# The shared expert's down product: in 32-column slices with every combine, or whole in the first round

## The reference, cut to what matters

```python
def moe(x, ...):                       # xt: 256 tokens x 1024
    ...                                # sigmoid scores, 8 of 64 experts for each token, gates
    # for each expert e, on the tokens that chose it:
    y = (silu(h @ w_gate[e]) * (h @ w_up[e])) @ w_down[e] * wt
    routed = segment_sum(y, token)
    shared = (silu(xt @ sh_gate) * (xt @ sh_up)) @ sh_down      # 256 x 256 @ 256 x 1024
    return routed + shared

x = layer_norm(ALPHA * x + moe(x), ln2_g[i], ln2_b[i])          # ALPHA = (2 * DEPTH) ** 0.25
```

## Time and profile before

| | before |
|---|---|
| time, median of 3 runs | 1450.87 us (1449.27 to 1454.12) |
| profiled execution | span 1450.8 us; the page gives no other time for it |
| TensorE busy with matmuls | 1404.1 us, 97% |
| TensorE weight loads | 875.4 us, 60% |
| VectorE busy | 555.3 us, 38% |
| ScalarE busy | 361.1 us, 25% |
| mean granted TensorE clock | 0.985 |
| DMA | 468.48 MB, mean 323 GB/s |

### The profile page before, as it was taken

One profiled execution on the slowest core, in us unless ns is written; L12 is line 12 of the kernel. 1 busy time (PEld: TensorE's weight loads), 2 busy tenths in 40 slices (PEclk: granted clock), 3 DMA queues, 4 the chain that ended last, 5 costly groups with the idle time before them and its releaser, 6 DMA issues.

```text
span 1450.8 us, 20457 instructions
## 1 busy us (share of the span) xinstructions
PE 1404.1 (97%) x7848; PEld 875.4 (60%) x7848; DVE 555.3 (38%) x1085; ACT 361.1 (25%) x611; POOL 10.2 (1%) x24
## 2 busy tenths in 40 slices
PE   8999999999999999995999999999999999999996
PEld 8986455555455555544999997455554555555553
DVE  5665232222233222234577666322222332222234
ACT  4422211122111112212544443121221111122110
POOL 0000000000000000000000000000000000000000
PEclk9999999999999999997999999999999999999998
DMA  9764799999999999964444455489999999999990
GB/s 332 269 262 200 305 384 396 403 394 394 410 392 392 397 399 401 398 232 186 175 175 160 173 238 205 157 333 387 393 397 405 383 410 398 389 399 396 392 378 30
DMA packets 82769, 468.48 MB, mean 323 GB/s; under 512 B 7065, under 2 KB 19481, under 8 KB 32674
## 3 DMA queue, kind: packets, MB, share of 16 engines
q1 hardware_dynamic: 81296, 463.50, 80.4%
q10 hardware_dynamic: 1426, 4.33, 0.8%
HBM read 466.76 MB, written 1.05 MB: 322 GB/s over the span
## 4 chain that ended last, share of the span: by engine, by line
PE 95%; DVE 2%; issue 1%; ACT 1%; DMA 0%; POOL 0%; DVEq 0%; POOLq 0%; ACTq 0%
PE ps L583 30%; PE ps L605 16%; PE ps L668 9%; PE ps L555 9%; PE ps L535 9%; PE ps L680 6%; PE ps L702 5%; PE ps L561 3%; PE ps L751 2%; PE ps L542 2%; PE ps L591 1%; PE ps L521 1%; PE ps L735 1%; PE ps L744 0%; DMA xT_in<-in_xT 0%
## 5 line engine op out<-in xcount | busy, mean ns | idle before, releaser
L583 PE MATMUL ps<-ring,xsT 128*64 128x512 f32 x2048 | 450.1, 592 | 1.2 <-DVE slot_tok L1053 1.2
L583 PEld LDWEIGHTS ps<-ring,xsT 128*64 128x64 f32 x2048 | 146.9, 137 | 292.6 <-issue 291.2
L605 PE MATMUL ps<-ring,hidT 128*64 128x512 f32 x1024 | 233.8, 598 | 2.3 <-ACT hidT L850 2.3
L996 DVE TENSOR_TENSOR ring_low<-ring,wh 128x1024 fp32r<-128x1024 f32 (+1 forms) x112 | 128.4, 1148 | 113.0 <-ACT wh L828 112.5
L1059 DVE SCALAR_TENSOR_TENSOR gated<-sig,slot_gate,ps 128x256 f32<-128x256 f32 x64 | 30.8, 481 | 364.7 <-ACT sig L846 364.7
L1068 DVE TENSOR_TENSOR yl<-ps,yh 128x512 fp32r<-128x512 f32 x128 | 88.5, 691 | 175.2 <-ACT yh L855 175.2
L828 ACT CAST wh<-ring 128x1024 fp32r<-128x1024 f32 (+1 forms) x112 | 110.5, 988 | 157.7 <-PE ps L668 70.6
L855 ACT CAST yh<-ps 128x512 fp32r<-128x512 f32 x128 | 75.0, 586 | 268.1 <-PE ps L605 268.1
L605 PEld LDWEIGHTS ps<-ring,hidT 128*64 128x64 f32 x1024 | 67.8, 136 | 114.5 <-issue 109.6
L535 PE MATMUL ps<-sel,xh 128*128 128x256 f32 x512 | 130.8, 296 | 4.3 <-DVE g_cols L1046 4.3
L846 ACT ACTIVATE sig<-ps 128x256 f32<-128x256 f32 x64 | 24.6, 384 | 401.8 <-PE ps L583 401.8
(11 more groups left out here) (149 smaller groups left out, 1418.8 us busy)
## 6 DMA issues: line engine op xcount, KB each, us to landing
ring<-in_w_gate SPq DMA_DIRECT2D x128, 1024.0 KB, 7.5
ring<-in_w_up SPq DMA_DIRECT2D x128, 1024.0 KB, 9.9
ring<-in_w_down SPq DMA_DIRECT2D x128, 1024.0 KB, 9.0
ring<-in_b_w_in SPq DMA_DIRECT2D x8, 3072.0 KB, 11.9
ring<-in_a_w_in SPq DMA_DIRECT2D x12, 1024.0 KB, 12.7
ring<-in_b_w_out SPq DMA_DIRECT2D x4, 3072.0 KB, 11.5
ring<-in_a_w_out SPq DMA_DIRECT2D x1, 3072.0 KB, 16.5
ring<-in_sh_gate SPq DMA_DIRECT2D x2, 1024.0 KB, 4.7
```

What stands on the lines that cost most here:

```text
L583: last = nc.tensor.matmul(ps[64 * half:64 * half + 64, p, :], xsT[:, c, (2 * p + half) * SLOTS:(2 * p + half + 1) * SLOTS], slot_gu(s)[:, ...
L605: last = nc.tensor.matmul(ps[64 * half:64 * half + 64, 4 + h, :], hidT[:, p, kk * P + 64 * half:kk * P + 64 * half + 64], slot_dn(s)[:, kk ...
L996: nc.vector.tensor_tensor(wl_n, w, wh_n.bitcast(FP32), ALU.subtract).then_inc(L[layer].wl_ready, 1)
```

## The change

The two 32-column products leave `combine`. Instead `shared_down(t)` computes, in round 0, 128 tokens x 1024 columns for each token half t, as four products of 512 columns (two column halves, two contraction steps) into PSUM banks 2 and 3: for t = 0 behind `down(0, 0)`, for t = 1 behind `slot_info` and ahead of `down(0, 1)`. The second waits for `acc_ready`, since it writes the same banks. VectorE then computes ALPHA * x + product for each half in one instruction over 1024 columns (`residual_and_shared`), both behind `select` and ahead of `take_info` in round 0. ScalarE's two scalings, the wait before round 1 and the memset go. The sums into `acc` are the same but for their order.

```diff
                                                     start=(p == 0 and part is yh),
-                                                    stop=(p == 1 and part is yl and not k.head_first))
-                    if k.head_first:
-                        for kk in range(HC):
-                            last = nc.tensor.matmul(ps[:, 2 + n % 2, bass.ds((i - 1) * SHARE, SHARE)],
-                                                    sh_hT[:, kk, t * P:(t + 1) * P],
-                                                    sh_dn[:, kk, bass.ds((i - 1) * SHARE + h * HALF, SHARE)],
-                                                    start=False, stop=(kk == HC - 1))
+                                                    stop=(p == 1 and part is yl))
                     last.then_inc(k.comb_done, 1)
...
+                def shared_down(t):
+                    if t == 0:
+                        pe.wait_ge(shared.sh_hT_ready, 1)
+                        pe.wait_ge(g.sh_dn, 16 * (k.layer + 1))
+                    else:
+                        pe.wait_ge(shared.acc_ready, t)
+                    for h in range(2):
+                        for kk in range(HC):
+                            last = nc.tensor.matmul(ps[:, 2 + h, :], sh_hT[:, kk, t * P:(t + 1) * P],
+                                                    sh_dn[:, kk, h * HALF:(h + 1) * HALF],
+                                                    start=(kk == 0), stop=(kk == HC - 1))
+                    last.then_inc(shared.sh_down, 1)
...
                     down(i, 0)
                     if not first:
                         gate_up(i, 1)
+                    elif shared:
+                        shared_down(0)
...
                         slot_info(k)
+                    if first and shared:
+                        shared_down(1)
                     down(i, 1)
...
-                if k.head_first:
-                    for t in range(TT):
-                        nc.scalar.mul(acc[:, t, :], x_tok[:, t, :], ALPHA).then_inc(L[k.layer].acc_ready, 1)
...
+                def residual_and_shared(t):
+                    dve.wait_ge(L[k.layer].sh_down, t + 1)
+                    last = nc.vector.scalar_tensor_tensor(acc[:, t, :], x_tok[:, t, :], ALPHA,
+                                                          ps[:, 2:4, :].rearrange("p a b -> p (a b)"), ALU.mult, ALU.add)
+                    if t == 0:
+                        last.then_inc(L[k.layer].acc_ready, 1)
+                    else:
+                        last.then_inc(k.comb_taken, 2)
...
                         select(k, i * QUAD + (first + QUAD))
+                    if start and k.head_first:
+                        residual_and_shared(0)
+                        residual_and_shared(1)
...
-                if k.head_first:
-                    dve.wait_ge(L[k.layer].acc_ready, TT)
...
-                nc.vector.memset(w_sum[:, 0:1], 0.0).then_inc(k.comb_taken, 2)
```

More of the change, by code:

```diff
@@ L58 @@
 NEG = -1e30
-SHARE = HALF // QUADS
 FILLS = [
@@ L259, in build @@
                            "xl_ready logits scored chosen ranks over sh_gu sh_sig sh_h sh_hT sh_hT_ready over_ranks over_rows first_done "
-                           "acc_ready ln2_rows ln2_var ln2_rstd x2_ready x2T_done x2T_ready") for i in range(DEPTH)]
+                           "acc_ready sh_down ln2_rows ln2_var ln2_rstd x2_ready x2T_done x2T_ready") for i in range(DEPTH)]
         B = sems("b", "ws_masked sums sums_ready v_gelu v_var v_rstd v_norm u_gelu spatial y_ready yh_ready yl_ready")
@@ L645, in experts @@
                 quad(0, first=True)
-                if shared:
-                    pe.wait_ge(shared.sh_hT_ready, 1)
-                    pe.wait_ge(g.sh_dn, 16 * (k.layer + 1))
                 with pe.Fori(1, k.steps - 1) as i:
```

## The result

The changed kernel takes 1403.24 us (median of 4 runs, 1400.72 to 1405.51) against 1452.49 (median of 4, 1449.27 to 1455.53): ratio 0.9662, 95% interval 0.9641 to 0.9684. It is 3.4% faster. The forecast was 1409 with a range of 1404 to 1422. The medians lie 49.3 us apart: the profiled execution of the changed kernel was the slowest of its four.

A forecast was written before the change was run, and what follows sets the result against it. The prediction took TensorE's unbroken chain of products, slices included, to bound the kernel, with DMA second. Rounds saved 48.0 us, round 0 cost 6.7, last combines saved 0.7: 42.0 off 1450.8, forecast 1409 us, range 1404 to 1422.

The forecast's parts named there:

- The slices stand on the path: Rounds 1 to 15: removing the slices from TensorE's chain saves 1.60 us a round, 48.0 us over 30 rounds.
- The switch of format into the down product: Combine into down product, each round: could cost 0.20 us, leaving 1.40 us saved a round.
- The clock in the rounds: Rounds 1 to 15: no fall of the granted clock was forecast there; only round 0's clock was priced.
- Round 0: Whole product added, once per layer: round 0 grows by 3.35 us, or 4.75 if the clock still falls.
- Pause and clock: Round 0: the product's first half covers 2.11 us of TensorE's pause; the clock stays up, giving back 1.40 us.
- VectorE's cover: Combine, third quarter: VectorE's first add is done 0.16 us before needed; a 0.3 us stall a round had 8%.
- The last combine: Last combine of each layer: VectorE sets the pace, so only the first quarter's 0.36 us is won.
- The transfers: Weight DMA in rounds: 427 GB/s possible, 29.5 us a round, 0.6 us to spare; floor at present round had 4%.
- 48.0 - 6.7 + 0.7 = 42.0 us off the span: Whole kernel: rounds' gain, round 0's cost and last combines' gain take the span from 1450.8 to 1408.8.
- From the span to the time: Whole kernel: the median of the runs lies 0.1 us above the span, so 1408.8 was given as 1409.
- The range: Whole kernel: 1404 to 1422 us, meant to leave out no more than two in ten.

The follow-up runs named there:

- e5: Kernel before without the 32-column products, nothing in their place, so the shared expert's down product is missing: 1396.55 us, ratio 0.9617.
- e3: Changed kernel with 68 instructions more in the branch that isn't taken, so the code behind it lies as in the kernel before: 1409.86 us, one run.
- e4: Changed kernel with 128 instructions more in the branch that isn't taken, a third code position: 1401.86 us, one run.
- e8: Changed kernel with the combine's products of the low halves yl left out, to push the transfers: 1381.69 us, one run.
- e10: Changed kernel once more, unchanged: 1402.22 us, ratio 0.9664.
- e11: Changed kernel with 128 instructions more in the branch that isn't taken (e4 again, timed over 5 runs): 1402.34 us, ratio 0.9663.
- e7: Changed kernel with the first half of the shared product moved behind the first gather of round 0: 1410.53 us, ratio 0.9710.
- e9: Changed kernel with the first four weight fills of layer 1's mixer held until the products behind the branch are done: 1412.67 us, one run.
- e1: Kernel before once more, unchanged: 1450.32 us, one run.
- e2: Kernel before with 188 instructions more in the branch that isn't taken, to move the code behind it: 1441.62 us, one run.
- e6: Kernel before with slices of 64 overlapping columns in place of 32: 1453.35 us, one run.
- e12: e11 with four products of the identity in each layer's last round, where TensorE waits for ScalarE's copy: 1402.39 us, ratio 0.9659.

## Why the prediction was right in kind and wrong in size

- **The slices stand on the path: right.** 1.65 us a round (24.8 / 15, and e5 gives the same), against 1.60; 49.6 us for 30 rounds against 48.0. The term was mis-sized by 1.6; most of it is the transposes, 0.23 us a round where they were 0.30. The switch of format into the down product, which I feared at 0.20, costs nothing: the down product starts 1.89 us behind the third quarter and takes its 3.58.
- **The clock in the rounds: missed.** In the last round of layer 1 it fell, 1.7 us:

```profile
1380.60:1384.00 3.40, 3.27 (x8) 1.00 (x10) 0.00 (x0) 0.08 (x1) 0.00 (x0) 0.50 0.00 0
```

  Without slices it fell in the last round in 11 of 18 layers: in layer 1 of the kernel after, e3, e4, e8, e10 and e11, in layer 0 of e7, in both of e5 and e9. In the 8 layers with slices (before, e1, e2, e6) it never did. In e12, with the wait of 0.45 us filled, it stayed up in both layers of one execution; as it also did in 7 of the 18 layers without the filling, this is a hint and no more. Why the slices, a round earlier, kept it up is open.
- **Round 0: right.** +3.27 and +3.23 us, against 3.35. The sum is a little better than its terms: the product took 7.17 us in place of 6.86, and the gathers gave back 1.56 in place of 1.40. Pause and clock came back as forecast, and e7 shows that both depend on the place of the product's first half.
- **VectorE's cover: right, by nothing.** I gave it 0.16 us. After the change the third quarter starts 0.05 us behind the end of the first add, as in e8, where it does wait for it. So the cover is used up, but no stall shows: the piece of the transposes ahead of it takes 0.23 us, less than the 0.30 before. e8 shows that it is the next bound.
- **The last combine: right in kind,** -0.54 and -0.57 us, against -0.35 each.
- **The transfers: right in the verdict, wrong in the margin.** I took 427 GB/s from a stretch with a backlog for what they can do. e8 shows 422. A round of 30.03 us stands 0.2 us above the floor of 29.8, not 0.6. The Trainium skill's HBM limit of 358 GB/s ("DMA: Bandwidth & Descriptors", Specifications), which that row works out as half of what two cores share, does not bound this program on one core, whose rounds move 399 to 422; its ceiling of 435 is not reached.
- **The step that failed:** "48.0 - 6.7 + 0.7 = 42.0 us off the span". The sum held only the stretches that the edit touches and took all others as unchanged. Between the layers the changed kernel won 3.2 us in the profiled pair and 5.4 in the second, since taking 69 instructions a layer out of TensorE's program moved the code behind the branch off a place where two fetches stand ahead of the product (e2, e3). The piece of 11.56 us of "issue" stood in the chain of the kernel before, and I didn't ask what it waits for. Another 1.25 us at the start is a stretch of low clock that was 6.8 us long in one execution of the kernel before and 3.4 in another: luck, and within what its runs scatter. The terms of the 47.0: rounds -49.6, round 0 +6.5, last combines -1.1, clock in the last round +1.7, between the layers -3.2, start -1.25.
- **From the span to the time: wrong too, and in the other direction.** The prediction added 0.2 us to the span of 1408.8, from the median of other executions. In every run with both figures the time is 1.7 to 1.8 us above the span (1405.51 and 1403.8 for the changed kernel). That would have put the forecast at 1410.5; the changed kernel's median is 7.3 below it, of which 5.0 are the sum's and 2.3 the profiled execution's distance from its median.
- **The range** reached 5 us below the forecast, for costs on the path alone. Nothing in it stood for what moves when a program gets shorter. That the median lies below it by 0.8 us, and not inside, is less than the runs scatter (1400.72 to 1405.51), but also less than the 3.2 us between the layers that the sum left out.

## What to carry to other kernels

A small product cost a price per record here that twice the columns did not raise: work that is cut into slices to hide it in a loop pays that price in every slice, and is cheaper whole, put where the engine waits anyway; there it may also keep the clock up. Where a kernel jumps over a large branch while weights stream, look at the unexplained "issue" in the chain and at the instruction queue: here an edit that only changed the length of the program moved that pause by 4 to 6 us, either way, and a comparison of two versions should be corrected for it before it is explained. And a rate read from a busy stretch is no ceiling; push one experiment past it and watch the time to landing.

## What the runs showed of the hardware

- The rate of weight transfers of 1 MB on one core levelled at 422 GB/s in e8, the same in 10 slices of 40 in a row, while their median time to landing grew from 11.4 to 17.6 us.
- Fetches of 16 KB on the instruction queue followed each other in 3.1 us with DMA engines at a share of 0.02 (e9) and in 5.7 to 6.0 with weights streaming. Whether the first product behind a jump came after one or two of them went with the place of the target: 8.4 to 11.0 us of pause at 3742, 3870 and 3999, 13.9 to 14.7 at 3810 and 3811.
- Float32 products of 64 columns took as long as those of 32: four records and the four of the next quarter took 0.39 + 0.98 us (e6) and 0.36 + 1.01 us.
- A pause of 2.1 us in round 0 was followed by half clock in 10 of 12 cases (before, e1, e2, e5, e6 and e7, two layers each), at 1.5 to 1.65 us each; with the pause filled, in none of the profiled executions.
